# A mask addition by heads, and a bias spread, convolution taps and norm sums in other places, in a two-block network kernel

## What is computed

```python
def first_block(x, ...):
    h = concat(meta, x)                                   # 272 x 1024
    z, xbc, dt_raw, conf_in = split(rmsnorm(h, norm_mix_w) @ w_in)
    y_ssd = ssd_mixer(z, xbc, dt_raw, ...)                # scan, gate by silu(z), norm of 4 groups
    y_conf = conformer_conv(conf_in, ...)                 # conv over 31 steps, layer norm, silu
    h = h + concat(y_ssd, y_conf) @ w_out
    h = h + peer_ffn(rmsnorm(h, norm_ffn_w), w_query, keys, w_down, w_up)
    return rmsnorm(h, norm_final_w)[:, 16:]

def second_block(x, ...):
    h = concat(meta_2, x)
    for layer in range(2):
        h = h + 0.5 * swiglu(rms_norm(h, ln_ffn1), ffn1_wi, ffn1_wo)
        mix = diff_attention(...) if layer == 0 else dsa_attention(...)
        h = h + mix @ w_out
        h = h + 0.5 * swiglu(rms_norm(h, ln_ffn2), ffn2_wi, ffn2_wo)
    return h[:, 16:]
# diff_attention, layer 0:
#   bias = rel_bias[bucket(pos[None, :] - qpos[:, None])]   # 16 (two maps of 8) heads
#   logits = q @ k * scale + bias;  p = softmax(where(visible, logits, -1e30))
```

## Time and profile before

| | us |
|---|---|
| median of 3 runs | 2488.09 (2488.03 to 2491.16) |
| the profiled execution | 2490.17 |
| its span, first to last instruction | 2488.3 |
| PE busy (matmuls) | 2286.5, 92% |
| PE busy (weight loads, beside the matmuls) | 2086.0, 84% |
| DVE busy | 1697.3, 68% |
| ACT busy | 1169.0, 47% |
| POOL busy | 228.8, 9% |
| mean granted clock of PE | 0.949 of full |

### The profile page before, as it was taken

The page is one execution under the profiler, slowest core; times in us unless marked ns, Lnnn a source line. Parts: engine busy times, 40 slices in busy tenths (PEclk is TensorE's granted clock), DMA queues, the critical chain, the costliest instruction groups (busy, mean ns, idle before and its releaser), DMA issues.

```text
span 2488.3 us, 42956 instructions
## 1 busy us (share of the span) xinstructions
PE 2286.5 (92%) x15436; PEld 2086.0 (84%) x15436; DVE 1697.3 (68%) x3067; ACT 1169.0 (47%) x1652; POOL 228.8 (9%) x124
## 2 busy tenths in 40 slices
PE   6987999999978999999699988799999998778999
PEld 5985899999977788888699976489999996447999
DVE  6799569999769655556776675556667755844774
ACT  4431257777768555555465443324443442232443
POOL 4650000000027000000200100010010010001000
PEclk8997999999999999999899996599999999989999
DMA  4437456665530566656455531045565562202555
GB/s 130 149 105 130 140 165 185 185 186 186 185 119 0 161 186 188 190 186 187 133 176 172 184 119 51 1 136 176 171 185 176 169 188 83 65 4 77 185 182 180
DMA packets 107935, 359.40 MB, mean 144 GB/s; under 512 B 12976, under 2 KB 21552, under 8 KB 107728
## 3 DMA queue, kind: packets, MB, share of 16 engines
q1 hardware_dynamic: 105792, 354.04, 46.0%
q10 hardware_dynamic: 2064, 4.33, 1.5%
HBM read 351.90 MB, written 6.42 MB: 144 GB/s over the span
## 4 chain that ended last, share of the span: by engine, by line
PE 81%; DVE 13%; issue 2%; DMA 2%; ACT 1%; POOL 0%; DVEq 0%; SPq 0%; ACTq 0%
PE ps L506 18%; PE ps L508 18%; PE ps L507 18%; PE ps L804 14%; PE ps L495 2%; PE ps L732 2%; DVE hot_keys L1449 1%; DVE ps L1214 1%; DVE big L1561 1%; PE ps L1034 1%; DMA ring<-in_mix_out_dram 1%; DVE hw_hi L1096 1%; DVE big L1695 1%; DVE big L1633 1%; PE ps L973 1%
## 5 line engine op out<-in xcount | busy, mean ns | idle before, releaser
L506 PE MATMUL ps<-hw_hi,w_hi 128*128 128x272 f32 (+1 forms) x3104 | 896.6, 289 | 54.9 <-DVE ring_lo L403 21.7
L508 PE MATMUL ps<-hw_hi,ring_lo 128*128 128x272 f32 (+1 forms) x3104 | 892.6, 288 | 0.0
L507 PE MATMUL ps<-hw_lo,w_hi 128*128 128x272 f32 (+1 forms) x3104 | 891.3, 287 | 0.0
L397 ACT ACTIVATE w_hi<-ring 128x1024 fp32r<-128x1024 f32 x612 | 646.7, 1058 | 514.5 <-DMA ring<-in_ffn_in_dram 186.7
L403 DVE TENSOR_TENSOR ring_lo<-ring,w_hi 128x1024 fp32r<-128x1024 f32 x572 | 702.9, 1230 | 211.0 <-ACT w_hi L397 207.6
L506 PEld LDWEIGHTS ps<-hw_hi,w_hi 128*128 128x128 f32 x3104 | 593.8, 191 | 61.1 <-issue 55.6
L508 PEld LDWEIGHTS ps<-hw_hi,ring_lo 128*128 128x128 f32 x3104 | 593.4, 191 | 0.0
L507 PEld LDWEIGHTS ps<-hw_lo,w_hi 128*128 128x128 f32 x3104 | 592.1, 191 | 0.4
L804 PE MATMUL ps<-w_hi,hid_parts 128*128 128x512 f32 x1024 | 280.6, 396 | 2.3 <-DVE hid_parts L1476 2.3
L804 PEld LDWEIGHTS ps<-w_hi,hid_parts 128*128 128x128 f32 x1024 | 193.6, 189 | 47.8 <-issue 2.5
L506 PE MATMUL ps<-gated_hi,w_hi 128*128 128x272 f32 (+1 forms) x704 | 201.7, 287 | 3.6 <-DVE big L1520 3.6
(11 more groups left out here) (355 smaller groups left out, 2576.4 us busy)
## 6 DMA issues: line engine op xcount, KB each, us to landing
ring<-in_ffn_in_dram SPq DMA_DIRECT2D x176, 512.0 KB, 3.5
ring<-in_down_dram SPq DMA_DIRECT2D x128, 512.0 KB, 3.5
ring<-in_up_dram SPq DMA_DIRECT2D x128, 512.0 KB, 3.5
ring<-in_ffn_out_dram SPq DMA_DIRECT2D x96, 512.0 KB, 3.5
ring<-in_a_in_dram SPq DMA_DIRECT2D x24, 512.0 KB, 3.5
ring<-in_xbc_dram SPq DMA_DIRECT2D x16, 512.0 KB, 3.5
ring<-in_conf_dram SPq DMA_DIRECT2D x16, 512.0 KB, 3.5
ring<-in_mix_out_dram SPq DMA_DIRECT2D x16, 512.0 KB, 3.5
```

The costliest lines, as they stand in the source:

```text
L397: nc.scalar.activation(w_hi[:, u % RING, :], ring[:, u % RING, :], ACT.Copy).then_inc(hi_done, 1)
L506: nc.tensor.matmul(bank_out, w_hi[:, b, w], hi(k0 + k), start=start and k == 0, stop=False)
L507: nc.tensor.matmul(bank_out, w_hi[:, b, w], lo(k0 + k), start=False, stop=False)
L508: last = nc.tensor.matmul(bank_out, ring_lo[:, b, w], hi(k0 + k), start=False, stop=stop and k == m - 1)
```

## The change

Eight things change, all of them in where and when work is done; the sums that are computed stay the same up to the order of additions.

1. POOL adds the mask to the bias in 16 instructions, one for each head, each behind one gated tile of ffn1, instead of one before ffn1.
2. The norms of ffn1 and of peer are summed by POOL and are no longer waited for ahead of the first unit, as the other five; ffn1's first group stands outside its loop, like that of the other ffns.
3. ACT stores `u_rows` once (34 KB) as `u_table` early, and spreads it to `bias_rows` from DRAM to DRAM just ahead of the one-hot stage, not from SBUF between the silus of z and the squares of the gated y.
4. Taps: 14 and not 11 behind each odd conf unit e from e = 7 on, 17 and not 16 ahead of the gated norm (the last call takes what is left).
5. PE does tile 6 of the first half of `mix_out` before the last mean matmul and tile 7 after the variances.
6. In the additions of `mix_out`, `a_out` and `b_out` the low part of the next stage's unit 0 stands ahead of the last gain, and not behind it.
7. DVE and ACT make the third query unit's parts before the peer norm's root.
8. ACT squares the first norm's tiles before it waits for the constants.

```diff
-        SUMMED = {n: i for i, n in enumerate(["a", "ffn2", "ffn3", "b", "ffn4"])}
+        SUMMED = {n: i for i, n in enumerate(["peer", "ffn1", "a", "ffn2", "ffn3", "b", "ffn4"])}
@@ PE
-            out_half(0, y_norm)
+            out_half(0, y_norm, range(6))
             for k in range(KD):
+                if k == KD - 1:
+                    out_half(0, y_norm, (6,))
                 pe.wait_ge(conf_done, k + 1)
                 last = nc.tensor.matmul(ps[:, 3, 0:SEQ], C("mean_d"), conf[:, k, :], start=k == 0, stop=k == KD - 1)
...
             last.then_inc(var_mm, 1)
-            out_half(1, mix_ready)
-            stats("peer", META)
+            out_half(0, y_norm, (7,))
+            out_half(1, mix_ready, range(KD))
             for e in range(16):
-                pe.wait_ge(hw_ready, 16)
-                straight("query", e, normed(META), SEQ)
+                straight("query", e, normed(META), SEQ, normed_before=None if e else 8 * NORM["peer"])
+                if e == 0:
+                    summed_stats("peer", META)
...
-                summed = f"ffn{f}" if f > 1 else None
-                if f == 1:
-                    stats("ffn1", c0)
-                    pe.wait_ge(hw_ready, 8 * n)
-                loop_8(f"ffn{f}_in", normed(c0), T - c0, summed, c0)
+                loop_8(f"ffn{f}_in", normed(c0), T - c0, f"ffn{f}", c0)
@@ DVE
@@ add_halves
+                    if j == KD - 1:
+                        low("query", 0)
                     dve.wait_ge(acc_free, OUT0[name] + j + 1)
                     gain(base, j, c0)
@@ add_single
-            def add_single(name, base, c0):
+            def add_single(name, base, c0, following):
...
                     gain(base, j, c0)
+                    if j == KD - 2:
+                        low(following, 0)
+                low(following, 1)
...
                 if e % 2:
-                    conv_taps(11)
+                    conv_taps(11 if e < 6 else 14)
...
-            conv_taps(16)
+            conv_taps(17)
...
             add_halves("mix_out", VEC["norm_ffn"], META)
-            first_lows("query")
+            low("query", 1)
+            low("query", 2)
             invert("peer", META)
             for e in range(16):
...
-                low("query", e + 2)
+                if e:
+                    low("query", e + 2)
@@ DVE, ffn
-                if f > 1:
-                    low(name, 2)
+                low(name, 2)
                 invert(f"ffn{f}", c0)
...
-                if f > 1:
-                    group(0, True)
-                with dve.Fori(1 if f > 1 else 0, FF_CHUNKS // 2) as it:
+                group(0, True)
+                with dve.Fori(1, FF_CHUNKS // 2) as it:
...
-            dve.wait_ge(bias_ready, 1)
+            dve.wait_ge(bias_ready, HEADS)
@@ ACT
+            squares("mix", 0, h_loaded, 32)
             act.wait_ge(con_loaded, 32)
-            squares("mix", 0, h_loaded, 32)
...
+            act.wait_ge(u_copied, 2)
+            act.dma_start(u_table, u_rows).then_inc(u_saved, 16)
...
-            act.wait_ge(u_copied, 2)
-            act.dma_start(bias_rows.rearrange("h (q r) -> h q r", r=REL), bc(u_rows, 1, P)).then_inc(u_spread, 16)
             for j in range(KD):
                 act.wait_ge(gated_y, j + 1)
...
+            high("query", 2)
             root("peer", META, EPS_1)
-            for e in range(16):
+            for e in range(1, 16):
                 high("query", e + 2)
-            act.wait_ge(u_spread, 16)
+            act.wait_ge(u_saved, 16)
...
+            act.dma_start(bias_rows.rearrange("h (q r) -> h q r", r=REL), bc(u_table, 1, P)).then_inc(u_spread, 16)
             act.wait_ge(slots_ready, 1)
@@ POOL
+            sum_squares("peer", META)
...
+            sum_squares("ffn1", 0)
             pool.wait_ge(mask_loaded, 16)
             pool.wait_ge(bias_loaded, 32)
-            nc.gpsimd.tensor_tensor(bias[:, :, :], bias[:, :, :], bc(mask[:, 0, :], 1, HEADS), ALU.add).then_inc(bias_ready, 1)
+            for hd in range(HEADS):
+                pool.wait_ge(gated_ready, hd + 1)
+                nc.gpsimd.tensor_tensor(bias[:, hd, :], bias[:, hd, :], mask[:, 0, :], ALU.add).then_inc(bias_ready, 1)
```

34 lines of the change are left out of this document (16 added, 18 removed).

## The result

The kernel after takes 2471.03 us in the median (2469.98 to 2472.53, 4 runs), the kernel before 2488.06 beside it (2486.88 to 2491.16, 4 runs): a ratio of 0.993, with a 95% interval of 0.9913 to 0.9947. It is 17.0 us faster; 22.5 was forecast, 2465.6 us, with a range of 2458 to 2476. The profiled execution took 2469.98 us, its span is 2468.1.

A forecast was written before the change was run, and what follows sets the result against it. PE was taken to bound the kernel, busy 2286.5 of 2488.3 us. Terms -12.9 + 0 - 6.4 + 1.6 - 2.8 - 2.0 = -22.5 took the median 2488.1 to 2465.6 us, range 2458 to 2476.

The forecast's parts named there:

- terms 5 and 6: Additions at b_out and a_out: low part moved earlier, unit 0 straight behind the last tile; -2.8 and -2.0 us.
- Term 1: Entry to ffn1: mask by heads removes the long GpSimd hold, POOL sums the norm; -12.9 us.
- the rule of the page: SBUF port sharing, at ffn1's entry: certain DVE instructions and GpSimd SBUF reads block each other until the first ends.
- Term 2: Inside ffn1: the 16 mask adds hold DVE subtractions up to 0.45 us, hidden by its waits; 0 us.
- the 1.45: Inside ffn1: the 1.45 us DVE waits for PE in a pair of units, expected to cover the adds.
- Term 3: Conf stage and mix_out: bias spread moved, more taps in DVE idle time, tiles 6 and 7 moved; -6.4 us.
- -4 (no gain from the taps): Weaker bound for the spread, taps and mix_out tiles together, if the taps bring nothing: -4 us.
- Term 4: Peer norm: POOL's sum replaces eight statistics matmuls but is ready later, and the fifth query unit waits longer; +1.6 us.
- what ends next is POOL's sum: Step at b_out and a_out: earlier sums finish statistics earlier, -3.7 and -2.5 us before low-clock deductions.

The follow-up runs named there:

- mask_alone: Kernel before with one edit, the mask added in 16 per-head instructions behind ffn1's gated tiles: 2475.41 us against 2490.11, ratio 0.9941.
- mask_one_late: Kernel after, but the mask added in one instruction behind the 16th gated tile of ffn1: 2486.24 us.
- no_mask: Kernel after without any mask addition, computing something else and serving only for timing: 2470.26 us.
- tiles_both: Kernel after with tile 7 of mix_out's first half also ahead of the last mean matmul: 2469.45 us.
- spread_back: Kernel after with the bias spread issued at its old place behind the silus of z, still reading the DRAM table: 2471.67 us.
- table_source: Kernel before with the bias spread at its old place but reading the small DRAM table: 2491.29 us against 2489.49, ratio 1.0005.
- lows_squares_back: Kernel after with low parts behind the last gain at a_out and b_out, and first norm's squares behind the constants wait: 2473.85 us.
- late_stats: Kernel after with statistics of peer, ffn2 and ffn4 behind the next stage's second unit, fourth unit's parts before the root: 2464.46 us, ratio 0.9897 against before.

## Why the prediction was right, and which terms were off

The time was right within its range, 5.5 us short of the likeliest value. The largest term had its mechanism right; terms 5 and 6, 4.8 us of the forecast's 22.5, had theirs wrong, and that the sum stays inside the range owes something to how wide the range is.

*Term 1, right, 1.4 us too small.* The mechanism is shown by mask_alone and mask_one_late. In the frame of the kernel before (4.15 us later) the gains ended at 1199.3, forecast 1199.8. DVE lost 3.4 us under the sums (h and gains took 13.3 us, and without the hold 9.9 before), forecast 3.9; the prediction read the seven sums as agreeing with the rule of the page only in part, and the last section shows that they agree in full. The sums were done in 6.30 us and not 7.8, and PE's clock was up again by the end of its first unit, so "less 1.0 since part of the next unit may now run at the low clock" did not come.

*Term 2, right:* 0.3 us by no_mask, and by the mechanism it names: the held subtraction gets 0.57 us longer, forecast 0.45, inside the 1.45.

*Term 3, right in its order of events, off in one size.* 3.5 us of VectorE's idle time were filled (waits of 2.72, 1.69 and 1.09 us ahead of the conf gates before, 1.48 and 0.52 after), 3.4 were forecast, and the means ended at 255.9, forecast 255.7. The step that failed is "PE idles 3.3 us before 255.2, so a part may run at half clock: +0.9". It idled 4.81 us, the pair of matmuls behind it took 1.22 us and the variances 5.83, where 0.70 and 3.72 are the times in tiles_both: 2.6 us. Hence -4.6 and not -6.4. The first addition to h came at 270.42, forecast 268.7. The bound "-4 (no gain from the taps)" does not follow from the term's own numbers: -6.4 + 3.4 is -3.0, which moves the upper end of the range to 2476.8. And the reading behind the spread was wrong, though it did not change the sum: not "it now goes ... just ahead of the one-hot stage" frees the mix_out loads, but that it reads DRAM (spread_back). Alone it brings nothing (table_source); it lets tiles 6 and 7 and the taps count.

*Term 4, right in size (+1.5), but partly by other waits, so the size is luck.* The wait for the sum came (2.56 us), with a wait of 1.70 for the low part of unit 0 that the forecast had not seen (the low stands behind the last addition there, not ahead of it); the wait for the fifth unit, forecast to grow, was gone, since PE reached it later. mask_one_late and spread_back, with the same code there, show the trade: they wait only 0.90 us for the sum and then 1.53 and 1.67 for the fifth unit. The step from the 0.5 us that the term's rows give (314.5 for 314.0) to +1.6 was an estimate without rows.

*Terms 5 and 6, wrong: -4.8 forecast, -0.1 found.* The step that failed is "what ends next is POOL's sum ... statistics done 2293.5 against 2297.24 before". The statistics do come earlier, by 1.7 us at their start and 1.3 at their end at a_out (forecast 2.5). But PE never waited for statistics before; they end nothing. What counts is how long PE stands or runs slowly. At a_out: before a wait of 3.75 and the first unit at the low clock for 3.1 us; after 0.53 + 2.79 = 3.32 of waits and the *second* unit at the low clock for as long, and DVE's low parts under the sums (3.49 us for two, 1.22 each elsewhere) stretch these from 7.82 to 8.44; with the lows put back (lows_squares_back) they take 7.79. The hole was moved by one unit, not filled. late_stats, which fills it, gets 2 to 3 us at each place.

*Not forecast:* -1.5 in the up stage, by a stretch of low clock in the kernel before behind a wait that both kernels have, and +0.5 in the one-hot stage. The -1.5 brings the result nearer to the forecast without having been foreseen.

The terms as found add up to -18.6 (the ledger's -20.2 less the 1.6 us of one execution at b_out); in the two sets of runs that have both kernels, the medians differ by 17.0 and 18.9.

## What to carry to other kernels

Before a wait is counted as gain, ask what is late next and what the clock does behind the new hole: here a wait of 7.65 us removed alone gave nothing, and two waits of about 4 us moved by one unit gave 0.1, while a second unit put into them gave 2 to 3 each. Here a long elementwise instruction on GpSimd was cheap in pieces that fit into VectorE's own waits, and cost its full length in one. A DMA that spreads a small table is judged by its source too: store it once and read it from DRAM.
